# Loading and splitting each unit of weights in two halves instead of in one piece

## The chip, the cores and the metric

The kernel runs on one core of a Trainium2 chip. The metric is the device time of one launch in microseconds, taken as the median of three runs. The profile shows one further execution on the same kind of core. Engines are named as in the profile: PE is TensorE's matmuls and PEld its weight loads, DVE is VectorE, ACT is ScalarE, POOL is GpSimd and SP is SyncE, which issues the transfers here.

## What is computed

Two transformer layers over a sequence of 512 tokens with 1024 features, everything in float32. Cut to what the time goes to:

```python
def first_block(x, ...):                 # linear attention and window attention side by side
    proj = rms_norm(x) @ w_in            # 1024 -> 7200 columns
    y_gla = gla_branch(...) @ w_o_gla
    y_swa = swa_branch(...) @ w_o_swa
    x = x + (sigmoid(gate_a) * y_gla + sigmoid(gate_b) * y_swa) @ w_out
    gu = rms_norm(x) @ w_ffn_in          # 1024 -> 2 * 2816
    return x + (silu(gu[:, :2816]) * gu[:, 2816:]) @ w_ffn_out

def second_block(x, mem, ...):
    x = x + 0.5 * rms_norm(swiglu(rms_norm(x)))          # FFN 1: 1024 -> 2 * 2816 -> 1024
    ...  # differential attention (8 heads) and a state-space scan (32 heads), gated and merged
    ...  # cross attention (4 heads) to 256 rows of memory
    return x + 0.5 * rms_norm(swiglu(rms_norm(x)))       # FFN 2
```

Nearly all of the time is in products of activations with weight matrices that are read from memory once, some 59 million numbers (448 units of 128 x 1024).

## The kernel before

**Products in three matmuls.** A float32 product is made of three matmuls in the type float32r: weights and activations are each split into a high part (the value rounded to float32r) and a low part (what is left). `multiply_chunk` (L195 to 203) adds high x high (L201), high x low (L202) and low x high (L203) into the same bank. Activations lie with features on the partitions, as 8 chunks of 128 features by 512 tokens, so a matmul has 128 x 128 weights and usually 512 columns. Some tiles are done for half of the tokens at a time; their matmuls have 256 columns.

**Units, tiles, slots.** A unit is the weights of up to 8 chunks for 128 output features: 128 partitions x 1024 columns, 512 KB. There are 448 of them. A tile of output in `acc0` or `acc1` takes one unit, or three in the down projections of the FFNs (8, 8 and 6 chunks, `DOWN`). Units go through two slots (k % 2) of three buffers: `w_raw` as loaded, `w_hi` and `w_lo`. A stage's units stand in a `Stream`, and every engine walks through the same list, two units ahead of TensorE where it prepares weights:

- SyncE (`load_unit`, L121) transfers unit k + 2 into `w_raw` when the low part of unit k has been made (`lo_done`, L135 to 138, and the same in the stages written out).
- ScalarE (`split_hi`, L146 to 157) waits until TensorE has used unit k (`used`) and unit k + 2 has landed (`loaded`), and writes `w_hi` with one operation (L156).
- VectorE (`split_lo`, L160 to 169) waits for it (`hi_done`) and writes `w_lo` with one subtraction (L167), which counts `lo_done` up.
- TensorE (`multiply_tile`, L177 to 192) waits for `lo_done` once before a unit's first matmul and counts `used` up with its last.

Each engine works through its own program in a fixed order. ScalarE and VectorE also do the kernel's other work (norms, softmax, gates, the evacuation of banks), and the calls of `split_hi` and `split_lo` stand at fixed places between it. The gate/up projections run in loops of 22 rounds (the first at 567 to 807 us of the trace); most other stages are written out.

**Stages named in the text.** The last down projection of FFN 1 of the second layer (`LAST`, L494 and L604 to 606, `units` of `last_down_units`) does four tiles of 512 columns and then four rows of features twice, for 256 tokens at a time: 8 tiles, from 1232 to 1307 us; its operand is `9_hid`. The kernel's last down projection does the same with two rows (4 tiles, from 2612 to 2649 us; operand `19_hid`). The cross attention has keys and values from the memory (256 columns; `mem_h`) and an output projection (`heads`) whose last four tiles are 256 columns wide. `13_mask` is a table of 128 x 512 that is loaded once.

## Time and profile before

| | |
|---|---|
| median of 3 runs | 2661.84 us (2660.87 to 2663.51) |
| the profiled execution | 2663.67 us, its span 2661.8 us |
| mean granted clock of TensorE | 0.994 |
| transfers | 252.43 MB, of which units of weights 446 + 2 transfers; 16 engines busy 29.7% |
| high parts (L156) | 446 operations, 465.0 us busy |
| low parts (L167) | 446 operations, 541.3 us busy |

The span goes from the first to the last instruction. Busy time counts an engine's instructions from start to end; neighbouring ones overlap by some tens of nanoseconds. An "idle time before" says how long the engine had nothing to do before the instruction, and the name behind it says which instruction's semaphore came last. A matmul of 512 columns is shown with 0.39 us, but the next one starts 0.23 us after it.

### The profile page before, as it was taken

How to read it: one execution, taken by the hardware profiler on the slowest of the kernel's cores; microseconds unless marked ns; L12 is line 12 of the kernel's file. 1: busy time of each engine (PE TensorE's matmuls, PEld its weight loads, DVE VectorE, ACT ScalarE, POOL GpSimd, SP SyncE). 2: the span in 40 equal slices, each digit the busy share in tenths (PEclk: the TensorE clock that was granted, in tenths of full speed). 3: DMA queues.
4: the chain of work that ended last, by engine and by line, in shares of the span. 5: the costliest groups of instructions: out<-in, count | busy, mean ns of one | idle time of the engine just before them, and what ended most of it. 6: DMA issues, size and time to landing. Idle time of an engine off the chain costs nothing. (4 is left out here: it accounts for less than half of the span.)

```text
span 2661.8 us, 33727 instructions
## 1 busy us (share of the span) xinstructions
PE 2593.5 (97%) x12698; PEld 2134.1 (80%) x12698; DVE 1367.8 (51%) x2007; ACT 1129.2 (42%) x1757; POOL 130.5 (5%) x96
## 2 busy tenths in 40 slices
PE   7999999999999999999999999999999999999997
PEld 5887778888888888888877767888888888888887
DVE  7554454454443344433655646777745554644424
ACT  5444544342332233223555544766643443532322
POOL 1000000010000000001000000111101101000001
PEclk9999999999999999999999999999999999999999
DMA  3222122223223322234412213333332322223334
GB/s 122 72 76 72 59 68 72 95 95 99 98 95 95 94 96 95 95 98 118 138 64 72 72 65 116 119 107 126 97 111 99 124 89 79 94 95 96 99 95 125
DMA packets 74416, 252.43 MB, mean 95 GB/s; under 512 B 8400, under 2 KB 11472, under 8 KB 74176
## 3 DMA queue, kind: packets, MB, share of 16 engines
q1 hardware_dynamic: 74304, 250.89, 29.7%
q8 instruction: 76, 1.25, 0.2%
q14 instruction: 36, 0.29, 0.0%
HBM read 248.69 MB, written 2.16 MB: 94 GB/s over the span
## 5 line engine op out<-in xcount | busy, mean ns | idle before, releaser
L156 ACT ACTIVATE w_hi<-w_raw 128x1024 fp32r<-128x1024 f32 (+2 forms) x446 | 465.0, 1043 | 1009.6 <-PE acc L203 958.8
L201 PE MATMUL acc<-h_hi,w_hi 128*128 128x512 f32 (+1 forms) x2184 | 874.1, 400 | 11.3 <-DVE w_lo L167 3.4
L203 PE MATMUL acc<-h_hi,w_lo 128*128 128x512 f32 (+1 forms) x2184 | 845.2, 387 | 0.0
L202 PE MATMUL acc<-h_lo,w_hi 128*128 128x512 f32 (+1 forms) x2168 | 838.3, 387 | 0.0
L167 DVE TENSOR_TENSOR w_lo<-w_raw,w_hi 128x1024 fp32r<-128x1024 f32 (+2 forms) x446 | 541.3, 1214 | 524.4 <-ACT w_hi L156 523.9
L201 PEld LDWEIGHTS acc<-h_hi,w_hi 128*128 128x128 f32 x2184 | 410.6, 188 | 114.1 <-issue 27.7
L203 PEld LDWEIGHTS acc<-h_hi,w_lo 128*128 128x128 f32 x2184 | 410.4, 188 | 85.1
L202 PEld LDWEIGHTS acc<-h_lo,w_hi 128*128 128x128 f32 x2168 | 408.1, 188 | 83.1 <-issue 5.5
L201 PE MATMUL acc<-9_hid_hi,w_hi 128*128 128x512 f32 (+1 forms) x440 | 155.5, 353 | 8.0 <-DVE w_lo L167 8.0
L202 PE MATMUL acc<-9_hid_lo,w_hi 128*128 128x512 f32 (+1 forms) x440 | 154.6, 351 | 0.0
L203 PE MATMUL acc<-9_hid_hi,w_lo 128*128 128x512 f32 (+1 forms) x440 | 154.6, 351 | 0.0
L201 PEld LDWEIGHTS acc<-9_hid_hi,w_hi 128*128 128x128 f32 x440 | 83.4, 190 | 21.5 <-issue 7.9
L698 DVE TENSOR_TENSOR 9_up_hid<-acc,11_rstd 128x512 f32<-128x512 f32 x44 | 30.4, 692 | 128.4 <-PE acc L203 128.4
L202 PEld LDWEIGHTS acc<-9_hid_lo,w_hi 128*128 128x128 f32 x440 | 83.5, 190 | 12.1
L203 PEld LDWEIGHTS acc<-9_hid_hi,w_lo 128*128 128x128 f32 x440 | 83.4, 190 | 12.1
L693 DVE TENSOR_TENSOR 9_gate_silu<-acc,11_rstd 128x512 f32<-128x512 f32 x44 | 30.4, 691 | 104.7 <-PE acc L203 96.0
L201 PE MATMUL acc<-19_hid_hi,w_hi 128*128 128x512 f32 (+1 forms) x220 | 76.8, 349 | 3.4 <-DVE w_lo L167 3.4
L202 PE MATMUL acc<-19_hid_lo,w_hi 128*128 128x512 f32 (+1 forms) x220 | 76.2, 347 | 0.0
L203 PE MATMUL acc<-19_hid_hi,w_lo 128*128 128x512 f32 (+1 forms) x220 | 76.2, 346 | 0.0
L2636 DVE SCALAR_TENSOR_TENSOR 16_conv<-16_conv_in,small,16_conv 128x512 f32<-128x512 f32 x72 | 54.4, 756 | 30.7 <-ACT 16_conv L2523 29.0
L375 POOL TENSOR_TENSOR ssq<-ssq,11_sq 128x512 f32<-128x512 f32 x16 | 22.9, 1433 | 888.0 <-ACT 11_sq L364 888.0
L201 PE MATMUL acc<-heads_hi,w_hi 128*128 128x512 f32 (+1 forms) x160 | 56.8, 355 | 4.4 <-issue 2.0
(431 smaller groups left out, 3481.1 us busy)
## 6 DMA issues: line engine op xcount, KB each, us to landing
w_raw<-in_w_gu SPq DMA_DIRECT2D x132, 512.0 KB, 3.4
w_raw<-in_w_down SPq DMA_DIRECT2D x60, 512.0 KB, 3.6
w_raw<-in_w_ssd SPq DMA_DIRECT2D x40, 512.0 KB, 3.5
w_raw<-in_w_swa SPq DMA_DIRECT2D x28, 512.0 KB, 3.5
w_raw<-in_w_gla SPq DMA_DIRECT2D x24, 512.0 KB, 3.4
w_raw<-in_w_da SPq DMA_DIRECT2D x24, 512.0 KB, 3.5
w_raw<-in_w_ssd_out SPq DMA_DIRECT2D x24, 512.0 KB, 3.4
w_raw<-in_w_xa SPq DMA_DIRECT2D x24, 512.0 KB, 3.5
```

Source lines behind the costliest of these rows:

```text
L156: c.nc.scalar.activation(c.w_hi[:, k % 2, 0:chunks * P], c.raw[:, k % 2, 0:chunks * P], ACT.Copy).then_inc(c.hi_done, 1)
L167: c.nc.vector.tensor_tensor(c.w_lo[:, k % 2, 0:chunks * P], c.raw[:, k % 2, 0:chunks * P], c.w_hi[:, k % 2, 0:chunks * P].bitcast(F32), AL ...
L201: pe.matmul(out, hi, x_hi[:, j, cols], start=first, stop=False)
L202: pe.matmul(out, hi, x_lo[:, j, cols], start=False, stop=False)
L203: return pe.matmul(out, lo, x_hi[:, j, cols], start=False, stop=final)
L375: pool.tensor_tensor(self.c.ssq[:], self.c.ssq[:], self.sq[:, par, :], ALU.add).then_inc(self.summed, 1)
L693: dve.tensor_tensor(gate, c.acc[0][:], root.rstd[:], ALU.mult).then_inc(gate_done, 1)
L698: dve.tensor_tensor(up, c.acc[1][:], root.rstd[:], ALU.mult).then_inc(c.acc_free[1], 1)
L2636: ins = dve.scalar_tensor_tensor(conv[:, n % 2, :], u[:, n % 2, k:k + S], small("ssd_conv_w_2", 24 * i + 6 * k + n), conv[:, n % 2, :], AL ...
```

## The change

A unit is treated as two halves by chunks: chunks 0 to 3 and 4 to 7 (of 6 chunks, 3 and 3). `unit_halves` gives their columns. Each half has its own transfer with its own semaphore (`loaded[slot][h]`), its own high operation and its own low operation. `hi_done` and `lo_done` now count halves, so all their targets are doubled.

SyncE waits for the low part of the same half of unit k before it loads that half of unit k + 2. Where the new unit has more chunks than the old one, the first half waits for both. ScalarE waits for `used` of the whole unit, then for either landing. TensorE waits for `lo_done` at a unit's first chunk and again at the first chunk of its second half (`wait_half`); five places that are written out without `multiply_tile` wait for the second half at once. Matmuls, their order and their operands stay the same.

```diff
@@ -91,7 +91,7 @@
     c.eps, c.subln_eps, c.log_half = (constants[:, n:n + 1] for n in range(3))
 
     c.acc = [ctx.enter_context(nc.psum_tensor(f"acc{i}", [P, S], F32)) for i in range(2)]
-    c.loaded = [ctx.enter_context(nc.semaphore(f"w_loaded{i}")) for i in range(2)]
+    c.loaded = [[ctx.enter_context(nc.semaphore(f"w_loaded{i}_{h}")) for h in range(2)] for i in range(2)]
     c.hi_done = ctx.enter_context(nc.semaphore("w_hi_done"))
     c.lo_done = ctx.enter_context(nc.semaphore("w_lo_done"))
     c.used = ctx.enter_context(nc.semaphore("w_used"))
@@ -117,8 +117,23 @@
         assert self.n % 2 == 0 and tiles % 2 == 0 and units[0][0] == units[1][0] == KC
 
 
-def load_unit(c, sp, slot, chunks, src):
-    sp.dma_start(c.raw[:, slot, 0:chunks * P], src).then_inc(c.loaded[slot], 16)
+def unit_halves(chunks):
+
+    half = (chunks + 1) // 2
+    return (0, slice(0, half * P)), (1, slice(half * P, chunks * P))
+
+
+def load_unit(c, sp, slot, chunks, src, free=None, old=KC):
+
+    for h, cols in unit_halves(chunks):
+        if free is not None:
+            sp.wait_ge(c.lo_done, free + (h if chunks <= old else 1))
+        sp.dma_start(c.raw[:, slot, cols], src[:, cols]).then_inc(c.loaded[slot][h], 16)
+
+
+def wait_half(c, pe, i, k, h):
+
+    pe.wait_ge(c.lo_done, 2 * (c.unit + k) + h + 1 + i * (2 * c.stream.n))
 
 
 def stream_loads(c, sp, stream, following, after=None):
@@ -133,9 +148,8 @@
                 continue
             chunks, src = ahead.units[(k + 2) % n if ahead is stream else k + 2 - n]
 
-            sp.wait_ge(c.lo_done, base + i * n + k + 1)
             at = i if k + 2 < n else (i + 1 if ahead is stream else 0)
-            load_unit(c, sp, k % 2, chunks, src(at))
+            load_unit(c, sp, k % 2, chunks, src(at), 2 * (base + k) + 1 + i * (2 * n), stream.units[k][0])
         if after is not None:
             after(i, last)
 
@@ -152,9 +166,9 @@
         return
     chunks = c.stream.units[(k + 2) % n][0]
     act.wait_ge(c.used, c.unit + i * n + k + 1)
-    act.wait_ge(c.loaded[k % 2], (c.unit // 2 + i * (n // 2) + k // 2 + 2) * 16)
-    c.nc.scalar.activation(c.w_hi[:, k % 2, 0:chunks * P], c.raw[:, k % 2, 0:chunks * P],
-                           ACT.Copy).then_inc(c.hi_done, 1)
+    for h, cols in unit_halves(chunks):
+        act.wait_ge(c.loaded[k % 2][h], (c.unit // 2 + i * (n // 2) + k // 2 + 2) * 16)
+        c.nc.scalar.activation(c.w_hi[:, k % 2, cols], c.raw[:, k % 2, cols], ACT.Copy).then_inc(c.hi_done, 1)
 
 
 def split_lo(c, dve, i, k, last=False):
@@ -163,10 +177,10 @@
     if last and k + 2 >= n and c.following is None:
         return
     chunks = c.stream.units[(k + 2) % n][0]
-    dve.wait_ge(c.hi_done, c.unit + i * n + k + 3)
-    c.nc.vector.tensor_tensor(c.w_lo[:, k % 2, 0:chunks * P], c.raw[:, k % 2, 0:chunks * P],
-                              c.w_hi[:, k % 2, 0:chunks * P].bitcast(F32),
-                              ALU.subtract).then_inc(c.lo_done, 1)
+    for h, cols in unit_halves(chunks):
+        dve.wait_ge(c.hi_done, 2 * (c.unit + k) + 5 + h + i * (2 * n))
+        c.nc.vector.tensor_tensor(c.w_lo[:, k % 2, cols], c.raw[:, k % 2, cols], c.w_hi[:, k % 2, cols].bitcast(F32),
+                                  ALU.subtract).then_inc(c.lo_done, 1)
 
 
 def wait_tile(c, eng, i, k):
@@ -181,8 +195,9 @@
     for p, source in enumerate(parts):
         k = k0 + p
         chunks = c.stream.units[k % c.stream.n][0]
-        pe.wait_ge(c.lo_done, c.unit + i * c.stream.n + k + 1)
         for j in range(chunks):
+            if j in (0, (chunks + 1) // 2):
+                wait_half(c, pe, i, k, int(j > 0))
             if norm is not None:
                 norm.ready(pe, first_chunk + j)
             mm = multiply_chunk(c, pe, k, t, j, source, cols, p == 0 and j == 0, p == len(parts) - 1 and j == chunks - 1)
@@ -611,7 +626,7 @@
         for n, m in ((0, 0), (1, 0), (0, 1), (1, 1)):
             if m == 0:
                 wait_bank_free(c, pe, 0, n)
-                pe.wait_ge(c.lo_done, c.unit + n + 1)
+                wait_half(c, pe, 0, n, 1)
             for j in range(KC):
                 pe.wait_ge(h_lo_done, KC * m + j + 1)
                 mm = multiply_chunk(c, pe, n, n, j, (c.h_hi, c.h_lo), HALVES[m], j == 0, j == KC - 1)
@@ -978,8 +993,9 @@
             act.activation(SQ[k % 4], c.x[:, k, :], ACT.Square).then_inc(square, 1)
 
         def weight_hi(u):
-            act.wait_ge(c.loaded[u], 16)
-            act.activation(c.w_hi[:, u, :], c.raw[:, u, :], ACT.Copy).then_inc(c.hi_done, 1)
+            for h, cols in unit_halves(KC):
+                act.wait_ge(c.loaded[u][h], 16)
+                act.activation(c.w_hi[:, u, cols], c.raw[:, u, cols], ACT.Copy).then_inc(c.hi_done, 1)
 
         def root(out, src, width, sum_done, log, done, n):
             act.wait_ge(sum_done, n + 1)
@@ -1972,8 +1989,7 @@
             chunks, src = ahead.units[u]
             if k == places["k", H - 1]:
                 steps.store(sp)
-            sp.wait_ge(c.lo_done, c.unit + k + 1)
-            load_unit(c, sp, k % 2, chunks, src(0))
+            load_unit(c, sp, k % 2, chunks, src(0), 2 * (c.unit + k) + 1, c.stream.units[k][0])
             if k == 1:
                 sp.wait_ge(c.used, c.unit + 1)
                 sp.dma_start(mask[:], causal).then_inc(tables_in, 16)
...
```

The two other stages that are written out (L2416, L2812) change as the last piece above does, and four more waits of TensorE as the one at L614.

ScalarE's order in the 256-column tiles of the last down projection of FFN 1, before; `11_sq` is the square of a finished tile for the norm:

```order
432 L427 ACTIVATE 11_sq<-part_attn 128x256 [waits 12_summed,acc_free0]
433 L156 ACTIVATE w_hi<-w_raw 128x768 [waits w_loaded1,w_used]
434 L156 ACTIVATE w_hi<-w_raw 128x1024 [waits w_loaded0,w_used]
435 L156 ACTIVATE w_hi<-w_raw 128x1024 [waits w_loaded1,w_used]
436 L427 ACTIVATE 11_sq<-part_attn 128x256 [waits 12_summed,acc_free1]
```

The same place with the change (its lines are counted in the changed file, where L156 is L171 and L427 is L442):

```order
541 L442 ACTIVATE 11_sq<-part_attn 128x256 [waits 12_summed,acc_free0]
542 L171 ACTIVATE w_hi<-w_raw 128x384 [waits w_loaded1_0,w_used]
543 L171 ACTIVATE w_hi<-w_raw 128x384 [waits w_loaded1_1]
544 L171 ACTIVATE w_hi<-w_raw 128x512 [waits w_loaded0_0,w_used]
545 L171 ACTIVATE w_hi<-w_raw 128x512 [waits w_loaded0_1]
546 L171 ACTIVATE w_hi<-w_raw 128x512 [waits w_loaded1_0,w_used]
547 L171 ACTIVATE w_hi<-w_raw 128x512 [waits w_loaded1_1]
548 L442 ACTIVATE 11_sq<-part_attn 128x256 [waits 12_summed,acc_free1]
```

Three operations between two squares became six, and the second of each pair waits only for its own landing.

VectorE's order at the same place, before, where the copy evacuates the bank of a finished tile:

```order
470 L731 COPY part_attn<-acc 128x256 [waits w_used]
471 L167 TENSOR_TENSOR w_lo<-w_raw,w_hi 128x1024 [waits w_hi_done]
472 L167 TENSOR_TENSOR w_lo<-w_raw,w_hi 128x768 [waits w_hi_done]
473 L167 TENSOR_TENSOR w_lo<-w_raw,w_hi 128x1024 [waits w_hi_done]
474 L731 COPY part_attn<-acc 128x256 [waits w_used]
```

With the change (L167 is L182, L731 is L746):

```order
501 L746 COPY part_attn<-acc 128x256 [waits w_used]
502 L182 TENSOR_TENSOR w_lo<-w_raw,w_hi 128x512 [waits w_hi_done] x2
503 L182 TENSOR_TENSOR w_lo<-w_raw,w_hi 128x384 [waits w_hi_done] x2
504 L182 TENSOR_TENSOR w_lo<-w_raw,w_hi 128x512 [waits w_hi_done] x2
505 L746 COPY part_attn<-acc 128x256 [waits w_used]
```

The copies stand where they stood, with six subtractions between them instead of three.

TensorE's order around the fifth chunk of the first full unit of that stretch, before and with the change (L201 is L216):

```order
2834 L202 MATMUL acc<-9_hid_lo,w_hi 128x256
2835 L203 MATMUL acc<-9_hid_hi,w_lo 128x256
2836 L201 MATMUL acc<-9_hid_hi,w_hi 128x256
2837 L202 MATMUL acc<-9_hid_lo,w_hi 128x256
2838 L203 MATMUL acc<-9_hid_hi,w_lo 128x256
2839 L201 MATMUL acc<-9_hid_hi,w_hi 128x256
```

```order
2840 L217 MATMUL acc<-9_hid_lo,w_hi 128x256
2841 L218 MATMUL acc<-9_hid_hi,w_lo 128x256
2842 L216 MATMUL acc<-9_hid_hi,w_hi 128x256 [waits w_lo_done]
2843 L217 MATMUL acc<-9_hid_lo,w_hi 128x256
2844 L218 MATMUL acc<-9_hid_hi,w_lo 128x256
2845 L216 MATMUL acc<-9_hid_hi,w_hi 128x256
```

The matmul on the fifth chunk's high part now waits for `lo_done`; nothing is moved.

## Rows read from the trace of the kernel before

**Rows 1.** The page: busy us (share of the span) and instructions of each engine.

```profile
PE 2593.5 (97%) x12698; PEld 2134.1 (80%) x12698; DVE 1367.8 (51%) x2007; ACT 1129.2 (42%) x1757; POOL 130.5 (5%) x96
```

**Rows 2.** TensorE's waits: who waited for whom, us in total, times, longest.

```profile
PE acc L201 <- DVE w_lo L167: 18.2, 20, 2.1
...
PE 6_bank L1997 <- DVE 13_v L2168: 0.2, 1, 0.2
```

**Rows 3.** Groups of matmuls by shape: xcount, busy us, mean ns, idle before us.

```profile
L201 PE MATMUL acc<-h_hi,w_hi 128*128 128x512 f32 x2120 | 851.9, 402 | 8.8 <-DVE w_lo L167 3.4 <-PEq L3599 2.8 <-DVE h_lo L2979 2.6
L201 PE MATMUL acc<-9_hid_hi,w_hi 128*128 128x256 f32 x176 | 51.2, 291 | 8.0 <-DVE w_lo L167 8.0
L201 PE MATMUL acc<-heads_hi,w_hi 128*128 128x512 f32 x96 | 38.3, 399 | 3.8 <-issue 2.0 <-DVE w_lo L167 1.1 <-DVE heads_lo L3339 0.7
```

**Rows 4.** TensorE's waits for w_lo from 1232, from 2044 and from 2612 us.

```profile
PE acc L201 <- DVE w_lo L167: 8.0, 8, 2.1
PE acc L201 <- DVE w_lo L167: 3.4, 4, 1.1
PE acc L201 <- DVE w_lo L167: 3.4, 4, 1.5
```

**Rows 5.** Stretches: us, busy by engine (x), granted clock, DMA share, GB/s.

```profile
567.00:807.00 240.00, 240.00 (x1059) 198.36 (x1058) 110.32 (x131) 76.49 (x93) 1.86 (x1) 1.00 0.30 96
1232.40:1307.00 74.60, 66.64 (x530) 65.11 (x529) 41.47 (x66) 33.24 (x50) 6.23 (x4) 0.98 0.52 154
```

**Rows 6.** TensorE around a unit's first chunk in the gate/up loop: start us, us.

```profile
1105.30 0.39 PE L203 MATMUL acc<-h_hi,w_lo 128*128 128x512 f32 x1
1105.53 0.39 PE L201 MATMUL acc<-h_hi,w_hi 128*128 128x512 f32 x1
```

**Rows 7.** One unit's preparation, from its transfer to its first matmul: start us, us.

```profile
1234.95 0.33 SPq L121 DMA_DIRECT2D w_raw<-in_w_down  x1
1238.67 1.06 ACT L156 ACTIVATE w_hi<-w_raw 128x1024 fp32r<-128x1024 f32 x1 [2.37 <-DMA w_raw<-in_w_down]
1239.76 1.23 DVE L167 TENSOR_TENSOR w_lo<-w_raw,w_hi 128x1024 fp32r<-128x1024 f32 x1 [2.47 <-ACT w_hi L156]
1240.00 0.28 PE L202 MATMUL acc<-9_hid_lo,w_hi 128*128 128x256 f32 x1
1240.12 0.28 PE L203 MATMUL acc<-9_hid_hi,w_lo 128*128 128x256 f32 x1
1241.13 0.36 PE L201 MATMUL acc<-9_hid_hi,w_hi 128*128 128x256 f32 x1 [0.74 <-DVE w_lo L167]
```

**Rows 8.** High and low parts by shape: columns as in rows 3.

```profile
L156 ACT ACTIVATE w_hi<-w_raw 128x1024 fp32r<-128x1024 f32 x414 | 438.3, 1059 | 926.8 <-PE acc L203 883.0 <-DMA w_raw<-in_w_down 30.8 <-DMA w_raw<-in_w_xo 4.8
L156 ACT ACTIVATE w_hi<-w_raw 128x512 fp32r<-128x512 f32 x2 | 1.2, 624 | 0.9 <-PE acc L203 0.9
L167 DVE TENSOR_TENSOR w_lo<-w_raw,w_hi 128x1024 fp32r<-128x1024 f32 x414 | 511.2, 1235 | 451.9 <-ACT w_hi L156 451.4 <-DVE 19_gate L3444 0.2
L167 DVE TENSOR_TENSOR w_lo<-w_raw,w_hi 128x512 fp32r<-128x512 f32 x2 | 1.4, 686 | 0.9 <-ACT w_hi L156 0.9
```

**Rows 9.** Landings of L121, 1232 to 1307 us; the transfer of L1979.

```profile
DMA to landing us min/median/max: 3.0/3.6/5.1
13_mask<-in_causal SPq DMA_DIRECT2D x1, 256.0 KB, 2.7
```

**Rows 10.** VectorE's low parts before a wait in the scan, in cross attention.

```profile
1761.53 1.22 DVE L167 TENSOR_TENSOR w_lo<-w_raw,w_hi 128x1024 fp32r<-128x1024 f32 x1
2234.00 1.22 DVE L167 TENSOR_TENSOR w_lo<-w_raw,w_hi 128x1024 fp32r<-128x1024 f32 x1 [0.40 <-ACT w_hi L156]
```

**Rows 11.** The longest wait's matmul, and a stretch (columns as in rows 5).

```profile
1279.05 0.36 PE L201 MATMUL acc<-9_hid_hi,w_hi 128*128 128x256 f32 x1 [2.12 <-DVE w_lo L167]
...
1280.60:1284.00 3.40, 3.40 (x18) 3.40 (x18) 1.97 (x5) 0.88 (x2) 0.00 (x0) 0.50 0.75 242
```

## What the change will do to the time

> **What bounds the kernel now.** I read the page's busy times first. TensorE is busy for 97% of the span [rows 1], so a change that leaves its matmuls alone can win back only its idle time and what follows from idle time. Then I read who ends TensorE's waits. The change is about the first row, the low part w_lo: 18.2 us in 20 waits, the longest 2.1 us. That view has 17 further rows, 35 waits, down to 0.2 us, which have other causes [rows 2]. Third, the groups of matmuls by shape. The waits for w_lo are not where most of the matmuls are: 8.0 us of them stand before 256-column matmuls on 9_hid, and before 512-column ones there are 3.4 us on h_hi and 1.1 us on heads_hi [rows 3]. By stretches it is 8 waits in the last down projection of the first FFN of the second layer (1232 to 1307 us), 4 with 3.4 us in the one at the kernel's end (256 columns too), and 4 in the cross attention [rows 4]. Of those last four, one is the 1.1 us before a 512-column matmul, so the other three have 2.3 us. In all: 13.7 us in 15 waits before 256-column matmuls, and 4.5 us in 5 waits before 512-column ones.
>
> Why there? In the gate/up loop, 240 us long, TensorE is busy for 240.00 us. In the 256-column stretch it is busy for 66.64 of 74.60 us [rows 5]. Its matmuls start 0.12 us apart there (1240.00 and 1240.12 in rows 7), so a unit of 8 chunks, 24 matmuls, lasts 2.88 us; at 512 columns the step is 0.23 us [rows 6] and a unit 5.5 us. A unit's preparation doesn't get shorter with it. One round of a slot [rows 7]: the transfer is issued at 1234.95, its landing releases ScalarE at 1238.67, the high part takes 1.06, the low part starts at 1239.76 and takes 1.23, and TensorE starts at 1241.13. That is 6.18 us, and two units of matmuls (a slot is used by every second unit) last only 5.76 us, or 5.04 us where one of them has 6 chunks. The raw slot becomes free only with the end of the low part, so the loop closes on itself and its length is what TensorE sees.
>
> **What the halves do to one round.** Durations of the operations are shown in both sizes: the high part 1059 ns at 1024 columns and 624 ns at 512, the low part 1235 and 686 ns [rows 8]. So from the start of the high part to the first low part's end it is 0.62 + 0.03 + 0.69 = 1.34 us, where it was 1.06 + 0.03 + 1.23 = 2.32 us: 0.98 us earlier. ScalarE makes the second high part while VectorE makes the first low one; the second low part ends at 1.34 + 0.69 = 2.03 us at the latest, still 0.29 us before the old end. The first transfer of the next unit is issued at the first end, so up to 0.98 us earlier too. Its landing: units took 3.0 to 5.1 us in that stretch, median 3.6; the one 256 KB transfer of 128 rows took 2.7 [rows 9]. I bound it by 2.7 and 3.6 and take 2.7 to 3.1.
>
> The new round is then 2.7 + 0.07 + 1.34 + 0.14 = 4.25 us, and with a landing no shorter than before 5.15 us. Both are under 5.76, and against 5.04 the worse one is late by 0.1 us. TensorE reaches a second half 12 matmuls, 1.44 us, after the first, and it is ready 0.69 us after it. Only landings near 5.1 us stay visible (up to 6.65 us, late by 0.9 to 1.6). I therefore take away 90% of the 15 waits. A wait costs more than its idle time: from 1240.12 to 1241.13 the start is 1.01 us apart, of which 0.12 is the usual step and 0.74 the idle time, so 0.15 us is restarting [rows 7]. 0.9 x (13.7 + 15 x 0.15) = **14.4 us**.
>
> The Trainium skill speaks on both sizes. Its page "DMA: Bandwidth & Descriptors", section "Anatomy of one DMA — SWDGE (gpsimd) path", gives a fixed 2.0 us and 436 GB/s on another kind of queue, which by my estimate is 3.2 us for 512 KB and 2.6 us for 256 KB, a saving of 0.6 us. The trace, with 3.6 and 2.7, is near both; by the page the 15 waits would still vanish.
>
> **The five waits at 512 columns.** Three are in the scan, where the low part stands behind VectorE's own work: the one at 1761.53 has no idle time before it, that at 2234.00 had 0.40 us until the high part came [rows 10]. There only the shorter low part helps, 1.23 - 0.69 = 0.54 us each, 1.6 us. The other two (at 1438 us, and the one that follows 2234.00) come from ScalarE's high part and gain 0.98 each, 2.0 us. Together **3.6 us**, their restarts stay.
>
> **The clock.** The longest wait ended at 1279.05, and from 1280.6 to 1284.0 TensorE's granted clock is 0.50, the lower level, 1.2 GHz, with 18 matmuls in 3.4 us instead of 18 x 0.12 = 2.2 us [rows 11]. Without the wait before it I expect the stretch to stay at 1.00: **1.2 us**.
>
> **What it costs.** (1) About 448 waits within units. The order shows that they hang on the existing matmul. A matmul that waits for a semaphore already reached is shown at a unit's boundary, 1105.30 to 1105.53: a step of 0.23 us like the others [rows 6]. I take 0. If each broke the flow like a real wait, it would be 0.15 us each. Behind a waiting matmul TensorE's whole queue stands, so this would all be on the path. In the four loops two register operations per round are added; the same kind stands there already, under a TensorE that is 240.00 of 240 us busy: 0. (2) ScalarE and VectorE get a fixed part twice: by durations 2 x 624 - 1059 = 0.19 us and 2 x 686 - 1235 = 0.14 us per unit. Times 446 that is 85 and 62 us of engine time at most, on engines busy 42% and 51% [rows 1]; 926.8 us of ScalarE's idle time lies just before the 1024-column high parts [rows 8]. VectorE idles 451.4 us for the high parts. It counts only where one of the 35 other waits has a unit's preparation ahead of it, between +0.33 us and, where VectorE was waiting for the high part, -0.29 us each. Bounds +11.6 and -10; I take +1.5, since most of those rows name work of attention and norms and the shorter pair works the other way. (3) SyncE issues 446 more transfers of 0.33 us, 147 us on a queue of its own. At the start two issues stand before the later parts of x, half a microsecond at most; I take 0.5. Behind SyncE's new wait for the second low part stand tables and rows of the scan, and behind ScalarE's new wait for the second landing stand the squares of the down projections; both come up to 0.29 us earlier than before, or at the same time. Costs: **2.0 us**.
>
> **Sum.** 14.4 + 3.6 + 1.2 - 2.0 = 17.2 us. The profiled execution took 2663.67 us (span 2661.8), the median of the runs is 2661.84; the sum from the one would be 2646.5, and from the median, which I use, 2644.6 us.
>
> **Rivals.**
> (A) *The second half becomes the wait, or the landing doesn't get shorter.* Two transfers share the same 16 engines, which in this stretch are busy half of the time [rows 5], and landings of up to 5.1 us are there already. Then each of the 15 waits keeps about 0.7 us, and the costs under (2) come to 4.5 us: 17.2 - 15 x 0.7 - 3.0 = 3.7 us gained, 2658 us, within what can't be told from no change. For it: the spread of landings. Against it: 1.44 us of matmuls cover the 0.69 us between the halves.
> (B) *The gain is there, and more.* All 20 waits go with their restarts, 18.2 + 3.0, the clock's 1.2, and the earlier ends of preparations take 0.29 us from a dozen of the other waits, 3.5: 26 us, 2636 us.
> (C) *Slower: the fixed part of an operation lands on the path.* Where ScalarE or VectorE feeds TensorE in attention, scan and norms, each unit adds 0.33 us. It decides from 17.2 / 0.33 = 52 of the 446 units on. With a quarter of them, 112, it is +37 - 17, 2682 us. Against it: the same view shows only 35 waits outside w_lo, so 112 would need new ones. The Trainium skill, page "VectorE: DVE Perf Modes", section "The TRN2 errata — SBUF-src ops pay a fixed extra latency per instruction", speaks against the change in this sense: many small tiles pay a fixed latency each, one large tile pays it once. The trace agrees that there is such a part (0.14 us for VectorE, above), but beside it the engine has idle time.
> (D) *Slower: a wait within a unit stops TensorE from loading weights ahead.* 448 x 0.15 = 67 us, less 17: 2712 us. The steps at a unit's boundary speak against it [rows 6].
>
> **Chances.** Forecast 0.60, (B) 0.15, (A) 0.16, (C) 0.06, (D) 0.03. A change of under 0.2%, 5.3 us, can't be told from none in this kernel. The forecast's own range is 2640 to 2651. The range of all reaches from (B), 2636, to (A), 2658. Faster by over 0.2%: forecast, (B) and a quarter of (A), 0.79; within 0.2%: 0.12; slower: 0.09.
>
> **What would show it.** After the change, w_lo should nearly vanish from TensorE's waits: under 4 us in total, and in the 256-column stretch at most two of the eight, with its length down from 74.6 to about 65 to 66 us and its clock at 1.00. The 256 KB landings should be 2.7 to 3.1 us. The matmul at a unit's fifth chunk should start 0.23 us after its predecessor in the gate/up loop, whose 240 us stay. Waits of the scan should be near 0.15 us. I'd be wrong if the stalls move to the fifth chunk (A), if waits for h_lo, pt or y grow by more than 5 us in sum (C), or if the gate/up loop gets longer (D).

## The result, and the profile after

The changed kernel takes 2639.64 us, the median of 4 runs (2638.49 to 2640.46), beside 2661.56 us (2660.87 to 2663.51) for the kernel before on the same chip: ratio 0.9911, interval 0.9899 to 0.9922, 21.9 us less. The forecast was 2644.6 us, range 2636 to 2658; the narrower range of the forecast alone, 2640 to 2651, is missed by 0.4 us. On two other chips the same kernel gave ratios of 0.9899 (0.9883 to 0.9916) and 0.9903 (0.9888 to 0.9918). The profiled execution of after took 2638.49 us with a span of 2636.5, so by spans the difference is 25.4 us. The two profiled executions are the longest of before and the shortest of after: what is worked out from the traces below adds up to 3.3 us more than the medians are apart.

The page after, busy us, share and count of each engine, against [rows 1]:

```profile
PE 2587.2 (98%) x12698; PEld 2130.9 (81%) x12698; DVE 1388.9 (53%) x2455; ACT 1169.9 (44%) x2205; POOL 123.0 (5%) x96
```

ScalarE and VectorE have 448 operations more and are busy 41 and 21 us longer. TensorE has the same 12698 matmuls in a shorter span.

TensorE's waits after (who waited for whom, us in total, times, longest), first of the whole span and then from 1740 to 1930 us, the scan. They answer to [rows 2]:

```profile
PE 1_b L870 <- DVE y_gla_lo L1135: 4.1, 1, 4.1
...
PE acc L216 <- DVE w_lo L182: 2.6, 6, 1.0
...
PE acc L216 <- DVE h_lo L2993: 1.8, 3, 1.1
```
```profile
PE acc L216 <- DVE w_lo L182: 0.5, 3, 0.2
```

The waits for w_lo went from 18.2 us in 20 to 2.6 us in 6: three of 0.15 to 0.16 us in the scan, one of 0.45 us at 1425.56, and two at the end of the kernel, 0.69 and 1.04 us. The wait for y_gla_lo at the start grew, from 3.1 to 4.1 us.

Groups of matmuls by shape, against [rows 3] (count, busy us, mean ns, idle before):

```profile
L216 PE MATMUL acc<-h_hi,w_hi 128*128 128x512 f32 x2120 | 852.0, 402 | 4.5 <-PEq L3613 2.5 <-DVE h_lo L2993 1.1 <-DVE w_lo L182 0.9
...
L216 PE MATMUL acc<-9_hid_hi,w_hi 128*128 128x256 f32 x176 | 49.9, 284 | 0.0
...
L216 PE MATMUL acc<-19_hid_hi,w_hi 128*128 128x256 f32 x88 | 25.4, 288 | 1.7 <-DVE w_lo L182 1.7
```

The 8.0 us of idle time before the 256-column matmuls on 9_hid are gone altogether. The same by stretches, against [rows 5] and [rows 11] (us, busy of PE, PEld, DVE, ACT and POOL where there are five, granted clock, DMA share, GB/s):

```profile
1232.40:1295.70 63.30, 63.30 (x530) 63.03 (x529) 44.02 (x90) 35.48 (x74) 4.41 (x4) 1.00 0.56 174
```
```profile
567.00:807.00 240.00, 240.00 (x1059) 1.00 0.29 96
1280.60:1284.00 3.40, 3.40 (x31) 1.00 0.50 141
```

The 530 matmuls of the stretch of 74.6 us now take 63.3, with TensorE busy for all of it. The gate/up loop is what it was. In the 3.4 us from 1280.6, where 18 matmuls ran at half the clock, there are now 31 (later ones of the same stage) at the full one.

The two halves at work in that stretch, against [rows 7] and [rows 8] (start us, us; then columns as in rows 3):

```profile
1238.32 1.15 ACT L171 ACTIVATE w_hi<-w_raw 128x512 fp32r<-128x512 f32 x2 [1.91 <-PE acc L218]
1238.98 1.30 DVE L182 TENSOR_TENSOR w_lo<-w_raw,w_hi 128x512 fp32r<-128x512 f32 x2 [1.93 <-ACT w_hi L171]
```
```profile
L182 DVE TENSOR_TENSOR w_lo<-w_raw,w_hi 128x512 fp32r<-128x512 f32 x828 | 545.3, 700 | 357.5 <-ACT w_hi L171 354.2 <-DVE 19_gate L3458 0.2 <-DVE x_res L699 0.2
L171 ACT ACTIVATE w_hi<-w_raw 128x512 fp32r<-128x512 f32 x828 | 476.7, 624 | 899.4 <-PE acc L218 893.4 <-ACT 16_z_silu L2559 2.8 <-DMA w_raw<-in_w_down 2.4
```

VectorE starts 0.66 us after ScalarE, where it was 1.09 us [rows 7], and ends 1.96 us after it, where it was 2.32. What ScalarE waits for has changed too: 1.91 us for TensorE to leave the w_hi buffer, where it was 2.37 us for the landing. The round through the raw buffer is no longer the longest one. The landings, here in 1226 to 1296 us, against [rows 9] (256 and 192 KB together; those of 256 KB alone have a median of 2.8):

```profile
DMA to landing us min/median/max: 2.3/2.7/4.0
```

At a unit's fifth chunk TensorE now has a wait, which is always met in the gate/up loop. The unit that began at 1105.55 reaches it at 1108.27 (start us, us):

```profile
1108.04 0.39 PE L218 MATMUL acc<-h_hi,w_lo 128*128 128x512 f32 x1
1108.27 0.39 PE L216 MATMUL acc<-h_hi,w_hi 128*128 128x512 f32 x1
```

Both kernels issue the same matmuls in the same order, so each can be compared with its twin. This is where after's start moves against before's, by before's time (worked out from the start of every matmul in the two traces):

| stretch of before, us | change, us | what is there |
|---|---|---|
| first matmul | -0.54 | x landed earlier in this execution |
| to 25 | +0.74 | the start |
| 25 to 1232 | -0.19 | of it 522 to 567: -0.33; the gate/up loop 0.00 |
| 1232 to 1307.5 | -11.77 | last down projection, 8 waits; -1.6 of it the clock, -0.45 the next stage's first matmul at 1307.98 |
| 1307.5 to 1559 | -0.86 | the wait at 1438 |
| 1559 to 1625 | -1.70 | one half-clock stretch fewer |
| 1625 to 1960 | -1.22 | scan, three waits of -0.54, and +0.4 where after's last half-clock stretch ends later |
| 2044 to 2141 | -2.45 | cross attention |
| 2141 to 2210 | -2.36 | the wait named h_lo at 2147.60 |
| 2210 to 2294 | -2.83 | cross attention's end |
| 2612 to 2649.5 | -2.00 | the end, four waits |

### The profile page after: what moved, and what is told of

Read it like the earlier page. It is cut to its first block and busy times, and to the rows that moved or that the text cites. A ratio compares the mean times of both kernels' runs of the same rounds, so it can differ in the third digit from the quotient of the medians.

```text
span 2636.5 us, 35870 instructions
## 1 busy us (share of the span) xinstructions
PE 2587.2 (98%) x12698; PEld 2130.9 (81%) x12698; DVE 1388.9 (53%) x2455; ACT 1169.9 (44%) x2205; POOL 123.0 (5%) x96
## 5 line engine op out<-in xcount | busy, mean ns | idle before, releaser
L171 ACT ACTIVATE w_hi<-w_raw 128x512 fp32r<-128x512 f32 (+2 forms) x892 | 506.5, 616 | 975.3 <-PE acc L218 968.2
L216 PE MATMUL acc<-h_hi,w_hi 128*128 128x512 f32 (+1 forms) x2184 | 874.2, 400 | 5.6 <-PEq L3613 2.5
L182 DVE TENSOR_TENSOR w_lo<-w_raw,w_hi 128x512 fp32r<-128x512 f32 (+2 forms) x892 | 577.7, 689 | 432.3 <-ACT w_hi L171 429.1
L216 PEld LDWEIGHTS acc<-h_hi,w_hi 128*128 128x128 f32 x2184 | 410.8, 188 | 108.5 <-issue 24.1
L216 PE MATMUL acc<-9_hid_hi,w_hi 128*128 128x512 f32 (+1 forms) x440 | 154.2, 350 | 0.0
L216 PEld LDWEIGHTS acc<-9_hid_hi,w_hi 128*128 128x128 f32 x440 | 82.7, 188 | 12.2 <-issue 0.2
L216 PE MATMUL acc<-19_hid_hi,w_hi 128*128 128x512 f32 (+1 forms) x220 | 76.7, 349 | 1.7 <-DVE w_lo L182 1.7
L390 POOL TENSOR_TENSOR ssq<-ssq,11_sq 128x512 f32<-128x512 f32 x16 | 25.2, 1576 | 887.2 <-ACT 11_sq L379 887.2
L216 PE MATMUL acc<-heads_hi,w_hi 128*128 128x512 f32 (+1 forms) x160 | 56.7, 354 | 3.0 <-issue 1.7
```

Of the source, the lines that this page charges most:

```text
L171: c.nc.scalar.activation(c.w_hi[:, k % 2, cols], c.raw[:, k % 2, cols], ACT.Copy).then_inc(c.hi_done, 1)
L182: c.nc.vector.tensor_tensor(c.w_lo[:, k % 2, cols], c.raw[:, k % 2, cols], c.w_hi[:, k % 2, cols].bitcast(F32), ALU.subtract).then_inc(c.l ...
L216: pe.matmul(out, hi, x_hi[:, j, cols], start=first, stop=False)
```

## The experiments

Two kinds of question were open. Which of the three parts of the change (operations in halves, transfers in halves, TensorE waiting for halves) gives how much? And what are the waits that are left? The line numbers of the edits are those of the changed kernel.

**One transfer a unit.** Operations in halves and TensorE's two waits stay.

```diff
-    for h, cols in unit_halves(chunks):
-        if free is not None:
-            sp.wait_ge(c.lo_done, free + (h if chunks <= old else 1))
-        sp.dma_start(c.raw[:, slot, cols], src[:, cols]).then_inc(c.loaded[slot][h], 16)
+    if free is not None:
+        sp.wait_ge(c.lo_done, free + 1)
+    sp.dma_start(c.raw[:, slot, 0:chunks * P], src).then_inc(c.loaded[slot][0], 16)
```

> One transfer per unit again, issued when both low parts are made; high and low operations in halves and TensorE's two waits as in the changed kernel. Theory 1 (a round gets shorter in three places: landing, the overlap of ScalarE's and VectorE's halves, TensorE's start at the half): the round is about 3.6 + 0.07 + 1.95 = 5.6 us, under 5.76 but over 5.04, so about two thirds of the gain stay, 2646 to 2650 us, and the 1.5 us waits for h_lo at 2147 stay away only if they come from the operations. Rival 2 (the shorter landing alone does it): 2658 to 2662 us. Rival 3 (TensorE's start at the half alone does it): 2640 us, as the changed kernel.

Measured: 2645.76 us (2644.25 to 2647.23), ratio 0.9931 (0.9915 to 0.9948). Its stretch of 256 columns:

```profile
1232.60:1299.70 67.10, 65.06 (x531) 63.43 (x529) 43.21 (x89) 35.12 (x74) 4.64 (x4) 1.00 0.57 166
```
```profile
PE acc L215 <- DVE w_lo L181: 1.8, 5, 0.7
```

7.5 us of the stretch's 11.8 come without any change in the transfers. The time is at the lower edge of the 2646 to 2650 expected.

**Two transfers alone**, on the kernel before. Both are issued behind the whole low part, ScalarE waits for both.

```diff
-    sp.dma_start(c.raw[:, slot, 0:chunks * P], src).then_inc(c.loaded[slot], 16)
+    half = (chunks + 1) // 2 * P
+    for cols in (slice(0, half), slice(half, chunks * P)):
+        sp.dma_start(c.raw[:, slot, cols], src[:, cols]).then_inc(c.loaded[slot], 16)
```

> The kernel before with two transfers of half a unit on one semaphore, both issued when the whole low part is made; one high and one low operation, one wait of TensorE. Theory 1: the pair lands 3.4 to 3.7 us after the first issue, no sooner than one transfer did; 2659 to 2664 us. Rival 2 (landing alone): 2640 to 2648 us. Rival 3: 2661 us.

Measured: 2666.75 us (2661.74 to 2670.76, 10 runs), ratio 1.0009 (0.9999 to 1.0019). 2659 to 2664 us were expected; the kernel before has 2663.96 on that chip, so there is no gain. The landings of 1232 to 1307 us, and the stretch:

```profile
DMA to landing us min/median/max: 2.4/2.8/4.3
```
```profile
1232.00:1307.50 75.50, 69.21 (x535) 67.28 (x534) 42.55 (x67) 33.36 (x50) 5.94 (x4) 0.95 0.49 153
```

The median landing is 2.8 us, but the second of a pair is issued 0.37 us after the first and lands 3.33 us (median) after the first one's issue; whole units took 3.6 in the median [rows 9]. So a pair hands ScalarE a whole unit only 0.3 us earlier, and the stretch gained 0.36 us. The waits for w_lo in it did fall, from 8.0 us in 8 to 6.1 in 6, but it holds two half-clock stretches of 3.4 us where before has one (the clock of 0.95, 0.98 in [rows 5]), and that took back about 1.7 us. Over the whole span these waits are 18.1 us, as they were 18.2 before: what the stretch gained was lost in the cross attention (4.7 us against 3.4).

**TensorE waits for all.** Transfers and operations stay in halves; both are waited for at a unit's first chunk.

```diff
-            if j in (0, (chunks + 1) // 2):
-                wait_half(c, pe, i, k, int(j > 0))
+            if j == 0:
+                wait_half(c, pe, i, k, 1)
```

> The changed kernel, but TensorE waits for both low parts at a unit's first chunk. Theory 1: the round of a slot (second landing 2.7, high 0.62, low 0.69) stays far under 5.04, so the transfer-bound waits stay away; the scan's three waits come back to 0.7 us and 1438 and 2235 gain 0.3 us less; 2641 to 2644 us. Rival 2: 2640 us. Rival 3: 2655 to 2661 us.

Measured: 2647.33 us (2645.60 to 2649.53), ratio 0.9936 (0.9919 to 0.9953), 3 us more than expected. TensorE's waits of the stretch, then of the scan:

```profile
PE acc L216 <- DVE w_lo L182: 0.5, 1, 0.5
```
```profile
PE acc L216 <- DVE w_lo L182: 2.3, 3, 0.8
```

In the stretch 9.7 of 11.8 us remain: the cycle is short enough without TensorE's second wait. In the scan each of three waits is 0.60 us longer than in the changed kernel, since the low part there stands behind VectorE's own work. The excess over the expectation is at one place: a wait of 3.19 us at 2044.80, for which the profile names no releaser ("issue"), where before has 2.02 us and the changed kernel 1.67, and around its end 6.8 us at half clock; together +3.8 us to before and 3.4 more than in the changed kernel. VectorE's row there names what the profile doesn't. First this kernel, then the changed one:

```profile
2041.26 3.44 DVE L182 TENSOR_TENSOR w_lo<-w_raw,w_hi 128x512 fp32r<-128x512 f32 x2
2044.80 0.77 PE L216 MATMUL acc<-heads_hi,w_hi 128*128 128x512 f32 x1 [3.19 <-issue]
```
```profile
2034.73 3.45 DVE L182 TENSOR_TENSOR w_lo<-w_raw,w_hi 128x512 fp32r<-128x512 f32 x2
2036.59 0.47 PE L216 MATMUL acc<-heads_hi,w_hi 128*128 128x512 f32 x1 [1.67 <-issue]
```

The pair of low parts stands beside GpSimd's subtractions for heads_lo and takes 3.44 us, where the whole low part took 1.91 at that place before. With one wait TensorE starts 0.10 us after the pair's end; with two it starts 0.10 us after the end of the first half, at 2036.49.

**The operations alone.** The fourth corner: one transfer, one wait, operations in halves (the two edits above together).

> The operations of the preparation in halves, and nothing else: one transfer a unit as before the change, ScalarE's and VectorE's operation each in two halves, and TensorE waits for both at its first chunk. It closes the square: one transfer with TensorE's two waits kept 5 to 6 us less than the changed kernel, two transfers with one wait 6 to 7 us less, and two transfers alone gained nothing on the kernel before. Theory 1 (three shares of one cycle from issue to TensorE that add up: the halves let VectorE begin at 0.62 us after ScalarE and not at 1.06, the transfers take 0.6 off the landing, the last half is 0.6 of TensorE's waiting): the gain on the kernel before is 8 to 14 us, a ratio of 0.9948 to 0.9970, with the waits named h_lo at 2147 and 2272 us gone as in the changed kernel. Rival 2 (each part works only with the other two): the ratio is above 0.998. Rival 3 (the halved operations are the whole gain, the other parts nothing): the ratio is below 0.994.

Measured: 2653.71 us (2650.62 to 2654.70), ratio 0.9961 (0.9947 to 0.9974). Its stretch and its waits there:

```profile
1232.00:1300.80 68.80, 64.90 (x526) 63.02 (x525) 43.35 (x89) 35.21 (x74) 4.39 (x4) 1.00 0.55 163
```
```profile
PE acc L215 <- DVE w_lo L181: 3.6, 3, 1.7
```

The same wait of 3.19 us and the same half-clock stretch are here, +3.8 us: the pair of low parts ends at 2045.96 and the matmul starts at 2046.05. Put together (ratio to before; change of 1232 to 1307.5 us):

| operations | transfers | TensorE | ratio | stretch, us |
|---|---|---|---|---|
| whole | halves | one wait | 1.0009 | -0.4 |
| halves | whole | one wait | 0.9961 | -5.8 |
| halves | whole | two waits | 0.9931 | -7.5 |
| halves | halves | one wait | 0.9936 | -9.7 |
| halves | halves | two waits | 0.9911 | -11.8 |

The ratios are from three chips, each against the kernel before on the same chip; the stretches are from single traces. The operations in halves alone give half of the stretch's gain, and every larger gain has them in it. Transfers in halves give 4 us more in the stretch behind halved operations, whose first end frees half of the raw buffer 0.69 us before the second; alone they gave 1.9 us less waiting there, which the clock took back, and nothing in the time. How much of the 4 us is the shorter landing and how much the earlier issue, no run separates. TensorE's second wait adds about 2 us in the stretch, 1.8 in the scan (three times 0.60) and 3.4 at 2044.80, which it spares TensorE the slow second half and the half-clock stretch.

**Four parts** instead of two, everywhere.

```diff
-    half = (chunks + 1) // 2
-    return (0, slice(0, half * P)), (1, slice(half * P, chunks * P))
+    at = [chunks // QUARTERS * q + min(q, chunks % QUARTERS) for q in range(QUARTERS + 1)]
+    return [(q, slice(at[q] * P, at[q + 1] * P)) for q in range(QUARTERS)]
```

> Units in four parts (2 + 2 + 2 + 2 chunks; 2 + 2 + 1 + 1 for six), with four transfers, four high and four low operations and four waits of TensorE. Theory 1: only 2.6 us of waits for w_lo are left to take, and the operations' fixed part is paid 2 x 446 x 2 times more (about 0.2 us on either engine per part, 0.7 us per unit in all) beside idle time: 2638 to 2644 us, with the start 1 to 2 us longer. If the fixed part or the waits within a unit were on the path (rivals C and D of the prediction): over 2655 us, and the gate/up loop longer than 240 us.

Measured: 2646.05 us (2644.59 to 2647.40), ratio 0.9932 (0.9915 to 0.9948). By shape, the gate/up loop, and a group of waits in the scan:

```profile
L185 DVE TENSOR_TENSOR w_lo<-w_raw,w_hi 128x256 fp32r<-128x256 f32 x1716 | 628.8, 429 | 392.7 <-ACT w_hi L174 389.5 <-DVE 19_gate L3462 0.2
```
```profile
567.00:807.00 240.00, 240.00 (x1059) 198.48 (x1058) 119.71 (x265) 89.10 (x227) 3.06 (x2) 1.00 0.32 96
```
```profile
PE 16_pst L2479 <- DVE 16_x_to_end L2699: 2.7, 6, 0.5
```

Slower than two parts, against the 2638 to 2644 us expected (the intervals of the ratios touch that of the first comparison, 0.9899 to 0.9922; the traces show where). VectorE's unit is now 4 x 429 = 1716 ns, where it was 1235 whole and 1400 in halves. It costs nothing in the gate/up loop, though TensorE waits three more times per unit there, but it shows where VectorE itself is awaited: the start (+2.6 us on before, +0.7 in the changed kernel) and the scan (2.7 us of waits that neither kernel had). The 256-column stretch gained 10.2 us where two parts gained 11.8. One half-clock stretch more than in the changed kernel, between 1560 and 1620 us, is luck.

**The order at the start.** VectorE makes unit 0's low part behind the splits of all eight chunks of y_gla.

```diff
-        weight_lo(0)
         raw_split(4)
         raw_split(5)
         raw_split(6)
         raw_split(7)
+        weight_lo(0)
```

> The changed kernel with one order changed at its start: VectorE makes the low half of unit 0 after it has split raw chunks 4 to 7 and not before them, so both low halves of unit 0 and the first of unit 1 stand together. In the changed kernel two of these operations took 1.77 and 1.75 us beside GpSimd's additions, against 0.68 alone, and the work behind them came 0.6 us later than before the change; TensorE's wait for y_gla_lo there was 4.073 us against 2.942. Theory 1 (the start's loss is this slow pair standing ahead of the splits): the loss up to 25 us goes from +0.74 to about 0 or below, and the time is 1 to 3 us under the changed kernel's on the same chip. Rival 2 (the loss is the first landing, which the order does not touch): the stretch to 25 us stays within 0.3 us of the changed kernel's. Rival 3 (moved, not removed: the slow pair is now late for TensorE's first matmuls with the low part): the first w_lo waits appear in the first 25 us, of 1 us and more.

Measured: 2637.88 us (2636.10 to 2637.89 in three runs) beside 2639.40 (2638.36 to 2640.39) for the changed kernel on that chip; ratios 0.9890 (0.9871 to 0.9910) and 0.9899. First the changed kernel in its first execution (in the one beside, the wait is 3.67 us and the half-clock stretch as long): VectorE, TensorE's matmul behind it, and a stretch (columns as above).

```profile
14.35 3.45 DVE L1141 TENSOR_TENSOR w_lo<-w_raw,w_hi 128x512 fp32r<-128x512 f32 x2
17.72 3.44 DVE L1135 SCALAR_TENSOR_TENSOR y_gla_lo<-x_res,small,y_gla_hi 128x512 fp32r<-128x512 f32 x2
...
19.53 0.80 PE L870 MATMUL 1_b<-y_gla_hi,1_lr_w_hi 128*128 128x512 f32 x1 [4.07 <-DVE y_gla_lo L1135]
```
```profile
17.90:24.70 6.80, 5.10 (x10) 3.16 (x11) 6.80 (x6) 1.22 (x3) 4.10 (x3) 0.50 0.14 48
```

Then the other order, TensorE and the same stretch:

```profile
16.43 0.51 PE L870 MATMUL 1_b<-y_gla_hi,1_lr_w_hi 128*128 128x512 f32 x1 [0.73 <-DVE y_gla_lo L1135]
18.14 0.50 PE L870 MATMUL 1_b<-y_gla_hi,1_lr_w_hi 128*128 128x512 f32 x1 [0.74 <-DVE y_gla_lo L1135]
...
23.31 0.47 PE L216 MATMUL acc<-y_gla_hi,w_hi 128*128 128x512 f32 x1 [0.81 <-DVE w_lo L1141]
```
```profile
17.90:24.70 6.80, 4.29 (x15) 2.66 (x16) 6.80 (x7) 1.48 (x3) 4.42 (x3) 1.00 0.06 14
```

One wait of 4.07 us became four of 0.7 and one of 0.8, and the clock stays at 1.00 where it was 0.50 for 6.8 us: 15 matmuls in the time of 10. The stretch to 25 us is 2.6 us shorter than in the changed kernel beside it (-1.41 against +1.15 to before), 2.0 to 2.2 shorter than in its two other executions. In the time 1.5 us are left of it; in the profiled executions a third half-clock stretch fell between 1553 and 1612 us here, where the changed kernel has two.

**The order at the end.** At the last column tile, two low parts go ahead of the residual's steps.

```diff
-                        steps(3, 0 if k == 8 * per else 3, 3 if k == 8 * per else 6)
+                        steps(3, 0 if k == 8 * per else 2, 2 if k == 8 * per else 5)
+                    if n == 9 and k == 9 * per:
+                        steps(3, 8, KC + 2)
...
-                    steps(3, 6, KC + 2)
+                    steps(3, 5, 8)
```

> The changed kernel with one order changed at its end: VectorE's low halves of the last unit are made ahead of steps of the residual's work that stood before them, and one group of steps moves one tile later. The changed kernel still waits 0.695 and 1.036 us for w_lo at 2614.52 and 2621.66. Theory 1 (these waits are VectorE's order alone, no longer a landing or the length of an operation): both waits go, the stretch 2612 to 2649.5 us is 1 to 2 us shorter, nothing else moves. Rival 2 (the landing or ScalarE's high half sets them): the waits stay within 0.2 us, or their name changes to h_lo or w_hi at the same length. Rival 3 (the moved steps are late at the very end): the stretch behind 2649.5 us is longer by what the waits gave.

Measured: 2637.77 us (2637.30 to 2639.54), ratio 0.9893 (0.9876 to 0.9909), 1.6 us below the changed kernel beside it. The end's stretch is 0.7 us shorter than there, but at most 0.1 us shorter than in two other executions with the old order (-2.59 us to before, against -2.50 and -2.56): the wait of 0.69 us varies by itself, 0.83, 0.20 and 0.14 in those three. Here it is gone, and one of 0.34 has come at the next unit. That of 1.04 stayed at 0.90, since VectorE still had three steps ahead of that low part. So of the 1 to 2 us expected between nothing and 0.7 came, and what the time shows beyond that, no trace explains.

**Both orders**: 

> The changed kernel with both orders changed, at the start and at the end, as a version to beat both kernels. If the two are independent, as their places 2600 us apart say, it is faster than the changed kernel on the same chip by the sum of the two single gains, 2 to 5 us; a half-clock stretch of 3.4 us that falls elsewhere may take or give 1.7 us.

Measured: 2636.96 us (2635.58 to 2637.51), ratio 0.9889 (0.9873 to 0.9906), 2.4 us below the changed kernel beside it. The two differences are 1.5 and 1.6 us alone. The traces support 2.0 to 2.6 us of it at the start and 0.1 to 0.8 at the end.

**The last unit first.** Both orders, and the low part that was still late now stands before the three steps.

```diff
                 if n == 8:
+                    split_lo(c, dve, 0, 9 * per, True)
                     steps(3, 5, 8)
```

> The version with both orders changed, and the last low part of all made before three more steps of the residual's work at the end: VectorE issued it 2.7 us after ScalarE's high half was done, and TensorE still waited 0.9 us for it. Theory 1 (VectorE's order alone): that wait goes and the stretch 2612 to 2649.5 us is 0.4 to 0.9 us shorter than with both orders; about 1 us in the time if nothing else moves, which timing can hardly tell. Rival 2 (the steps put behind it are late for TensorE or for the end): another wait of the same length appears before 2649.5 us, or the tail behind it is longer.

Measured: 2635.20 us (2634.56 to 2638.34), ratio 0.9896 (0.9881 to 0.9911), beside 2638.26 (2636.00 to 2639.61) for the changed kernel: 3.1 us less. By ratio the times can't tell it from both orders alone (0.9889); the trace can. TensorE with both orders only, and then with the last unit first:

```profile
2620.18 0.38 PE L216 MATMUL acc<-19_hid_hi,w_hi 128*128 128x256 f32 x1 [0.91 <-DVE w_lo L182]
```
```profile
2615.46 0.39 PE L216 MATMUL acc<-19_hid_hi,w_hi 128*128 128x256 f32 x1 [0.29 <-DVE w_lo L182]
...
2622.18 0.70 PE L3016 MATMUL 20_out<-ssq,ones 128*128 128x256 f32 x2 [1.43 <-DVE ssq L450]
```

The wait of 0.91 us is gone, nothing took its place, and the matmul's start came 1.06 us earlier; the end's stretch is 3.8 us shorter than before, where it was 2.6 with both orders. All waits for w_lo of L182 are down to 0.9 us in 3.

**The changed kernel again**, twice, beside the last two groups: 

> The changed kernel once more, unaltered, beside the three orders and the kernel before on one chip, since the kernel before gave 2661.56 us on one chip and 2663.96 on another. Expected: a ratio to the kernel before of 0.990 to 0.992, as before. It is the mark that the other three are read against; a ratio above 0.993 would say that a few of the us given to the change belong to the chip.

> The changed kernel once more as the mark on this chip for the other two. Expected: 0.990 to 0.992 of the kernel before.

Measured: 2639.40 us and ratio 0.9899, 2638.26 us and 0.9903. By stretches these two and the first execution differ by up to 0.6 us in the start, 0.4 in the last down projection, 0.8 from 1559 to 1625 us (where the half-clock stretches fall) and 0.6 at the end, and by less than 0.05 in cross attention.

## Why the prediction was right, and where it was not

**The 15 waits before 256-column matmuls: 14.4 us forecast, 13.9 measured.** The steps at the eight waits of 1232 to 1307 us are 0.90, 0.65, 0.76, 1.09, 0.82, 2.29, 0.51 and 2.11, together 9.1; the cross attention's three give 1.29, 0.80 and 0.70, the end 2.0. The mechanism is the one told. The stretch came out at 63.3 us and not at the 65 to 66 forecast: that was 74.6 less the idle time of 8.0 and the clock's 1.2, and I had left out the restarts (1.1), which the sum does hold; 0.4 more came from the clock and 0.5 from steps too small to name. The landing was at the lower bound that I used, 2.8 us for 256 KB. The Trainium skill's figures (page "DMA: Bandwidth & Descriptors", section "Anatomy of one DMA — SWDGE (gpsimd) path") had given an estimate of 2.6 us for this size and 3.2 for 512 KB; the trace has 2.8 and 3.6. But the lone transfers show that the saving is not 0.9 us of landing per unit; a pair together takes 3.33. My reading is that the shorter landing counts because its half is issued on its own, at the first end of VectorE; the runs show the two only together.

**The five waits at 512 columns: 3.6 us forecast, 3.4 measured.** Three of 0.54 in the scan, as worked out from 1.23 - 0.69; 0.87 at 1438 us, and 0.97 at 2235.37.

**The clock: 1.2 us forecast, 1.6 measured**, and another 0.9 us net between 1559 and 1630 us, where before had a half-clock stretch more (1.4 us at 1567). How many stand between 1550 and 1625 us differs from one execution to the next (two or three in this case's runs), so I count that as luck.

**Costs: -2.0 us forecast, about +5 measured.** This is the step that was mis-sized, with the wrong sign. The profiled executions are 25.2 us apart; 13.9, 3.4, 1.6 and 0.9 make 19.8. (The medians are only 21.9 apart; the 3.3 us between the two are how far executions of one kernel differ, so "about +5" holds for this pair of traces.) The start did cost: +0.74 us (0.59 to 1.15 in the other executions), the slow pair of low parts shown above. So did the slow pair at 2034.73: heads_lo stands behind it, and TensorE waited 0.44 us for it at 2040.03, where before had no wait. A wait within a unit cost nothing: 0.23 us at the fifth chunk, 0.00 over the gate/up loop, and still 0.00 with four parts. But preparations that other waits hang on ended earlier and not later. I had allowed for that, with -0.29 us each where VectorE waits for the high part, as a bound of -10, and chose +1.5. The largest were waits with another name. At 2147.60 TensorE waited for h_lo, so I filed it under norms. What stood ahead of it in the kernel before (start us, us):

```profile
2143.30 1.06 ACT L156 ACTIVATE w_hi<-w_raw 128x1024 fp32r<-128x1024 f32 x1 [1.34 <-DMA w_raw<-in_w_xa]
2144.26 0.71 ACT L2972 ACTIVATE h_hi<-x_res,small 128x512 fp32r<-128x512 f32 x1
2144.39 1.23 DVE L167 TENSOR_TENSOR w_lo<-w_raw,w_hi 128x1024 fp32r<-128x1024 f32 x1 [1.85 <-ACT w_hi L156]
...
2146.80 0.74 DVE L2979 SCALAR_TENSOR_TENSOR h_lo<-x_res,small,h_hi 128x512 fp32r<-128x512 f32 x1
...
2147.60 0.50 PE L201 MATMUL acc<-h_hi,w_hi 128*128 128x512 f32 x1 [1.40 <-DVE h_lo L2979]
```

ScalarE stood 1.34 us for the landing of a unit, h_hi was queued behind it, h_lo behind that and behind the unit's low part on VectorE. It is the same round through the raw buffer, seen through another tile's name. The same place after:

```profile
2123.87 1.14 ACT L171 ACTIVATE w_hi<-w_raw 128x512 fp32r<-128x512 f32 x2
2124.53 1.29 DVE L182 TENSOR_TENSOR w_lo<-w_raw,w_hi 128x512 fp32r<-128x512 f32 x2 [0.32 <-ACT w_hi L171]
2124.91 0.71 ACT L2986 ACTIVATE h_hi<-x_res,small 128x512 fp32r<-128x512 f32 x1
```

No wait for a landing is left, and the matmul came 1.56 us earlier. The step at this matmul is the same 1.56 us in every kernel with halved operations: one transfer, one wait, four parts, and the operations alone. With two transfers alone the wait got 0.84 us longer instead, and a half-clock stretch followed it. Smaller steps up to 2210 us add 0.8, the wait for h_lo at 2272.13 gave 1.2, and six waits elsewhere were 0.35 to 0.45 us shorter, 2.2 together. That is 5.8 us gained, 1.9 lost (0.74 at the start, 0.60 and 0.56 at 2055.40 and 2273.59 in cross attention), and 0.54 that the first landing gave, which is luck: 4.4 of the 5.4, the rest in steps too small to name.

**The rivals.** (A) falls: no wait for w_lo at a fifth chunk, and TensorE gets along in the stretch even where it waits for both halves. (B), 2636 us, came nearer than the forecast: 3.6 us from the measured median, where the forecast is 5.0 off, and 25.2 us of 26 in the profiled pair. Not all of it happened, since 6 of the 20 waits stayed, but the gain in other waits that sets it apart from the forecast is what was measured. The forecast lands near because its costs were small, not because their sign was right. (C): the fixed part is real, 2 x 700 - 1235 = 0.17 us a unit for VectorE, 0.48 with four parts. It reached the path only where the pair runs beside GpSimd (the start, and 0.60 us at 2055.40), and in the scan and the 256-column stretch only with four parts. The Trainium skill's rule (page "VectorE: DVE Perf Modes", section "The TRN2 errata — SBUF-src ops pay a fixed extra latency per instruction") is borne out by these prices; in the time it bears only on two parts against four, 0.9932 of before against 0.9899 to 0.9911, 6 to 9 us, of which one half-clock stretch is luck. (D) falls, by 0.00 us in the gate/up loop with one extra wait a unit and with three.

## What to carry to other kernels

Where a buffer's round (issue, landing, first operation, second operation, use) is longer than the compute that covers it, halve the operations first: it shortens the round by overlapping the two engines, and only behind that did halved transfers give anything in the time. Follow a wait back past the tile that names it: a wait for h_lo was a late weight transfer, with an innocent operation queued behind it, and a wait with no name ("issue") was a low part that ended 0.10 us before the matmul. Two parts were right here and four too many, because each part has a fixed price that is free under a busy TensorE and shows wherever the preparing engine is itself awaited; where that is, the order of its instructions is worth a look of its own (about 3 us in this kernel). And let the consumer wait for the first part alone: where the parts are slow, a wait for all of them cost 3.4 us at one place.

## What the runs showed of the hardware

VectorE beside GpSimd. The same low part of 128x512 takes 0.69 us alone and 1.77 and 1.75 us at 14.35 us, where GpSimd adds squares of 128x512 (1.55 us each); the whole part of 1024 columns took 2.31 us at that place before, so halving raised a unit's price there from 2.31 to 3.5. At 2034.73, beside GpSimd's subtractions, it raised it from 1.91 to 3.45. Starts of VectorE's 512-column operations were 1.7 us apart, like GpSimd's. The kernel before, GpSimd and then VectorE:

```profile
12.86 3.24 POOL L1297 TENSOR_TENSOR ssq<-ssq,1_grow 128x512 f32<-128x512 f32 x2
16.25 3.75 POOL L1297 TENSOR_TENSOR ssq<-ssq,1_sq 128x512 f32<-128x512 f32 x2
```
```profile
14.88 2.31 DVE L1124 TENSOR_TENSOR w_lo<-w_raw,w_hi 128x1024 fp32r<-128x1024 f32 x1
17.11 3.44 DVE L1119 SCALAR_TENSOR_TENSOR y_gla_lo<-x_res,small,y_gla_hi 128x512 fp32r<-128x512 f32 x2
```

The Trainium skill, page "GPSIMD Engine Reference", section "1. Specifications", says that GpSimd's memory interfaces are shared with VectorE, with contention for VectorE's instructions with two inputs in SBUF. By that rule each low part here is exposed, and the trace agrees at both places.

The clock. Within a wait of 4.07 us (15.46 to 19.53) TensorE's granted clock fell, at 17.9, to 0.50, its lower level of 1.2 GHz, for 6.8 us; with four waits of 0.7 us in the same stretch it stayed at 1.00. And a pair of transfers of half a unit, issued 0.37 us apart, landed 3.33 us after the first issue in the median, 0.5 us more than the median of one, at a DMA share of 0.49.
